# Expert weights loaded from the mixer's heads on, round 1's down weights ahead of the ranking, and the context's pieces some rounds later

## What is computed

```
for l in range(DEPTH):                        # first block, DEPTH = 2
    h = x * (1 + scale1) + shift1
    y = token_mixer(h, w_in[l], ..., w_out[l], cos, sin)
    x = layer_norm(ALPHA * x + gate1 * y, ln1_g[l], ln1_b[l])
    h = x * (1 + scale2) + shift2
    y = moe_ffn(h, router_w[l], router_bias[l], w_gate[l], w_up[l], w_down[l], ws_gate[l], ws_up[l], ws_down[l])
    x = layer_norm(ALPHA * x + gate2 * y, ln2_g[l], ln2_b[l])

def run_block(args):                          # in moe_ffn, for the tokens of one expert e
    e, toks, ws = args
    xb = x_pad[toks]
    hb = jax.nn.silu(xb @ w_gate[e]) * (xb @ w_up[e])
    return (hb @ w_down[e]) * ws[:, None]
```

## Time and profile before

| | |
|---|---|
| median of 3 runs | 2985.43 us (2981.14 to 2989.08) |
| the profiled execution | 2987.12 us, its span 2985.3 us |
| busy: PE, DVE, ACT, POOL | 2788.2, 1609.2, 766.0, 410.5 us |
| PE's chain of work that ended last | PE 75%, DVE 11%, DMA 9% of the span |
| moved by transfers | 717.28 MB, mean 240 GB/s |
| experts of layer 0 | about 281 to 794 us |
| experts of layer 1 | about 1044 to 1527 us |

### The profile page before, as it was taken

One profiled execution on the slowest core, in us unless ns is written; L12 is line 12 of the kernel. 1 busy time (PEld: TensorE's weight loads), 2 busy tenths in 40 slices (PEclk: granted clock), 3 DMA queues, 4 the chain that ended last, 5 costly groups with the idle time before them and its releaser, 6 DMA issues.

```text
span 2985.3 us, 65359 instructions
## 1 busy us (share of the span) xinstructions
PE 2788.2 (93%) x27428; PEld 2054.2 (69%) x27428; DVE 1609.2 (54%) x2814; ACT 766.0 (26%) x1408; POOL 410.5 (14%) x341
## 2 busy tenths in 40 slices
PE   7999999988989999998989899999998999899998
PEld 5768666655677856655567588844577888888973
DVE  3845333333463654444436478798757445555555
ACT  0122212121112133223213422200044424443210
POOL 1000000000000000000000036400023302444630
PEclk9999999999999999999999999999999999999999
DMA  9946999999984599999974035485430023001443
GB/s 392 374 184 239 407 395 410 391 421 420 408 336 143 221 391 418 414 407 420 420 283 155 1 129 172 168 314 191 141 120 4 4 91 135 4 18 32 156 168 113
DMA packets 102416, 717.28 MB, mean 240 GB/s; under 512 B 11648, under 2 KB 11936, under 8 KB 17888
## 3 DMA queue, kind: packets, MB, share of 16 engines
q1 hardware_dynamic: 98448, 700.03, 59.9%
q0 software_dynamic: 3664, 12.96, 1.3%
HBM read 710.06 MB, written 2.88 MB: 239 GB/s over the span
## 4 chain that ended last, share of the span: by engine, by line
PE 75%; DVE 11%; DMA 9%; ACT 3%; issue 2%; SPq 0%; POOL 0%; DVEq 0%; ACTq 0%; POOLq 0%
PE ps L229 16%; PE ps L1713 10%; PE ps L2267 9%; PE ps L2292 8%; DMA arena<-in_w_up 6%; DVE arena L162 5%; PE ps L3245 5%; PE ps L1742 5%; PE ps L2938 3%; PE ps L1810 2%; ACT arena L145 2%; PE ps L2660 1%; DMA arena<-in_w_in 1%; DVE arena L166 1%; DMA arena<-in_w_down 1%
## 5 line engine op out<-in xcount | busy, mean ns | idle before, releaser
L145 ACT ACTIVATE arena<-ps 128x512 f32<-128x512 f32 (+3 forms) x527 | 265.7, 504 | 1291.1 <-PE ps L229 276.6
L162 POOL TENSOR_TENSOR arena<-arena 128x512 f32<-128x512 f32 (+1 forms) x288 | 377.9, 1312 | 826.5 <-DVE arena L162 284.5
L229 PE MATMUL ps<-arena 128*128 128x256 f32 x2112 | 474.6, 385 | 16.0 <-DMA arena<-in_w_in 5.3
L229 PEld LDWEIGHTS ps<-arena 128*128 128x128 f32 x2112 | 402.5, 192 | 85.8 <-issue 11.2
L1713 PE MATMUL ps<-arena 128*32 128x256 f32 (+2 forms) x5120 | 395.2, 393 | 44.8 <-DMA arena<-in_w_up 33.8
L1713 PEld LDWEIGHTS ps<-arena 128*32 128x32 f32 (+2 forms) x5120 | 248.3, 121 | 194.5 <-issue 95.0
L162 DVE TENSOR_TENSOR arena<-ps,arena 128x256 f32<-128x256 f32 (+3 forms) x416 | 203.8, 490 | 236.9 <-PE ps L3245 88.4
L162 DVE TENSOR_TENSOR arena<-arena 128x512 f32<-128x512 f32 (+6 forms) x473 | 293.9, 621 | 61.0 <-PE ps L2292 36.0
L2267 PE MATMUL ps<-arena 128*128 128x256 f32 (+1 forms) x1792 | 298.5, 328 | 2.2 <-DVE arena L162 1.5
L2292 PE MATMUL ps<-arena 128*128 128x512 f32 x672 | 293.1, 593 | 2.5 <-DVE arena L162 2.5
L2267 PEld LDWEIGHTS ps<-arena 128*128 128x128 f32 x1792 | 270.0, 191 | 29.7 <-DVE arena L171 3.3
(11 more groups left out here) (292 smaller groups left out, 2908.4 us busy)
## 6 DMA issues: line engine op xcount, KB each, us to landing
arena<-in_w_gate SPq DMA_DIRECT2D x128, 1024.0 KB, 12.7
arena<-in_w_up SPq DMA_DIRECT2D x128, 1024.0 KB, 13.9
arena<-in_w_down SPq DMA_DIRECT2D x128, 1024.0 KB, 12.8
arena<-in_mlp SPq DMA_DIRECT2D x80, 1024.0 KB, 4.8
arena<-in_w_ada SPq DMA_DIRECT2D x48, 1024.0 KB, 13.1
arena<-in_ada SPq DMA_DIRECT2D x48, 1024.0 KB, 5.1
arena<-in_w_in SPq DMA_DIRECT2D x30, 1024.0 KB, 12.9
arena<-in_w_rkv SPq DMA_DIRECT2D x20, 1024.0 KB, 4.9
```

What stands on the lines that cost most here:

```text
L145: self.e.activation(out, in_, func, bias=bias, scale=scale, **more).then_inc(*self.done(key))
L162: self.e.tensor_tensor(out, a, b, op).then_inc(*self.done(key))
L229: ins = pe.matmul(out, a, b, start=start and i == 0, stop=stop and i == len(pairs) - 1)
```

## The change

- **Ahead of the end of the mixer.** The mixer's data is laid out anew, so that what lies in places 9 to 11 (`hT`, `PP`, `PT`, `qT`) is dead after the last pair of attention heads. After the first tile of `w_out`, `mixer_sp` now issues the shared gate and `FRONT`: both gates and both ups of round 0 and both gates of round 1, seven tiles, into places 5 to 11 (`load_apart` picks the place and leaves the ring's turn where it was). Places 9 to 11 wait for the heads' last values (`("mixer", l), "values", 3, 0`). The other three `w_out` tiles follow. Places 11 (both layers) and 10 (layer 0) are used for this alone and then go to the context.
- **Ahead of the ranking.** Then come the downs of round 0, the ups of round 1 and the downs of round 1; the last were issued in turn 1 before, behind the gates of round 2.
- **The context.** Its rows are loaded behind the gates of round 4 in layer 0 and not ahead of the ranking. In layer 1 the kept keys and values (0.5 and 0.25 MiB) follow the gates of round 2, and the kept queries (1 MiB) those of round 3. In layer 0 the squaring and scaling of the rows stand at the end of turn 3. `PIECE_ROUNDS` moves qkv 4 from turn 2 to 5, qkv 5 from 6 to 8, qkv 0 from 7 to 9, qkv 1 from 10 to 12, and the jobs between them alike; `HEAD_ROUNDS` starts in turn 3 instead of 1.

```diff
         def load(sp, key, used, src, parts=None, also=()):
...
-            if i >= NRING + NAPART and weights.fresh is not None:
-                ended(sp, weights.fresh, "pe", "act", "dve")
-                weights.fresh = None
...
+        def load_apart(sp, i, key, used, src):
+            turn, weights.turn, size, weights.size = weights.turn, i, weights.size, len(tiles)
+            load(sp, key, used, src)
+            weights.turn, weights.size = turn, size
...
+        FRONT = [(name, r, e) for name, r in (("w_gate", 0), ("w_up", 0), ("w_gate", 1)) for e in places_of(r)]
...
                 load(sp, ("w_bb", l, hf), ("y", l, hf * 4 + 3), D["w_bb"][l, hf])
-            for i in range(4):
+            load(sp, ("w_out", l, 0), ("mixed", l, 0, 1), D["w_out"][l, 0])
+            for i in range(NRING + NAPART, NRING + NEXTRA):
+                weights.used[i] = [(("mixer", l), "values", 3, 0)]
+            load_apart(sp, NRING, ("ws_gate", l), ("shared gate", l), D["ws_gate"][l])
+            for i, (name, r, e) in enumerate(FRONT):
+                load_apart(sp, NRING + 1 + i, (name, l, e), (name[2:], l, r), expert_rows(sp, name, l, e))
+            for i in range(1, 4):
                 load(sp, ("w_out", l, i), ("mixed", l, i, 1), D["w_out"][l, i])
...
-        PIECE_ROUNDS = {1: [("rows", 0), ("rows", 1), ("rows", 2)], 2: [("rows", 3), ("qkv", 4)], 3: [("keys", 0), ("keys", 1)],
-                        6: [("qkv", 5)], 7: [("qkv", 0)], 9: [("queries", 0)], 10: [("qkv", 1)], 12: [("queries", 1)], 15: [("qkv", 2)],
-                        16: [("queries", 2)], 17: [("qkv", 3)], 18: [("queries", 3)]}
+        PIECE_ROUNDS = {4: [("rows", 0), ("rows", 1), ("rows", 2)], 5: [("rows", 3), ("qkv", 4)], 6: [("keys", 0), ("keys", 1)],
+                        8: [("qkv", 5)], 9: [("qkv", 0)], 10: [("queries", 0)], 12: [("qkv", 1)], 13: [("queries", 1)],
+                        15: [("qkv", 2)], 16: [("queries", 2)], 17: [("qkv", 3)], 18: [("queries", 3)]}
...
-        for a, p in enumerate((1, 3, 7, 10, 14, 16, 18, 21)):
-            q = {3: 6, 7: 9, 10: 12}.get(p, p + 1)
+        for a, (p, q) in enumerate(((3, 4), (6, 7), (9, 10), (12, 14), (15, 16), (17, 18), (19, 20), (21, 22))):
...
         def moe_sp(sp, l):
-            weights.size, weights.turn, weights.fresh = NRING + EXTRA[l], NRING, ("mixer", l)
-            load(sp, ("ws_gate", l), ("shared gate", l), D["ws_gate"][l])
+            weights.size, weights.turn = NRING + EXTRA[l], 0
             for p, new, _, _ in rounds(l):
...
-                if new is not None:
+                if new is not None and new > 1:
                     for e in places_of(new):
                         load(sp, ("w_gate", l, e), ("gate", l, new), expert_rows(sp, "w_gate", l, e))
...
+                if new == 3 and l:
+                    sp.wait_ge(*at["gate", l, 1])
+                    sp.dma_start(CX.rows, kept[:, 0:2048]).then_inc(*tables["rows"]("c queries kept", 16))
+                if new == 4 and not l:
+                    sp.wait_ge(*at["gate", l, 1])
+                    sp.dma_start(CX.rv, D["ctx"].rearrange("(t p) n -> p t n", p=128)).then_inc(*tables["rows"]("rows", 16))
                 early_sp(sp, l, p, (0,))
-                if p >= 0:
+                if p >= 0 and p != 1:
                     for e in places_of(p):
                         load(sp, ("w_down", l, e), ("yd", l, p, 1), expert_rows(sp, "w_down", l, e))
...
+                if p == 0:
+                    for e in places_of(1):
+                        load(sp, ("w_down", l, e), ("yd", l, 1, 1), expert_rows(sp, "w_down", l, e))
```

More of the change, by code:

```diff
@@ L939, in __init__ @@
                 self.Zv = self.Z.rearrange("p (t n) -> p t n", t=2)
+                self.norms = arena[:, 6144:8192]
                 self.GSv = self.GS.rearrange("p (m t) -> p m t", m=16)
@@ L1116, in mixer_act @@
                 ended(act, ("moe", l - 1), "pe", "dve")
+                act.wait_ge(*at["c kept"])
             act.wait_ge(*mods(0, l, 0, 1))
@@ L1152, in mixer_dve @@
                 ended(dve, ("moe", l - 1), "pe", "act")
+                dve.wait_ge(*at["c kept"])
             else:
@@ L1566, in moe_sp @@
                     ended(sp, ("mixer", l), "pe", "act", "dve")
-                    if l:
-                        sp.wait_ge(*at["c kept"])
-                        sp.dma_start(gates[:, 0:1024], kept[:, 2048:3072]).then_inc(*tables["rows"](None, 16))
-                        sp.dma_start(CX.rows, kept[:, 0:2048]).then_inc(*tables["rows"]("c queries kept", 16))
-                    else:
-                        sp.dma_start(CX.rv, D["ctx"].rearrange("(t p) n -> p t n", p=128)).then_inc(*tables["rows"]("rows", 16))
@@ L1573, in moe_sp @@
                     sp.wait_ge(*at["ids", l])
-                    if l:
-                        sp.wait_ge(*at["scores", l])
-                        sp.dma_start(rw, kept[:, 3072:3584]).then_inc(*tables["rows"]("c values kept", 16))
-                if new is not None:
+                if new is not None and new > 1:
                     for e in places_of(new):
                         load(sp, ("w_gate", l, e), ("gate", l, new), expert_rows(sp, "w_gate", l, e))
+                if new == 2 and l:
+                    sp.wait_ge(*at["c kept"])
+                    sp.dma_start(gates[:, 0:1024], kept[:, 2048:3072]).then_inc(*tables["rows"](None, 16))
+                    sp.wait_ge(*at["scores", l])
+                    sp.dma_start(rw, kept[:, 3072:3584]).then_inc(*tables["rows"]("c values kept", 16))
@@ L1852, in moe_act @@
                 gather(0, k)
-            if not l:
-                context_rows_act(act, do)
             for p, new, Q, ks in rounds(l):
@@ L1883, in moe_act @@
                 early_act(act, do, l, p, 2)
+                if p == 3 and not l:
+                    act.wait_ge(*at["gate", l, 1])
+                    context_rows_act(act, do)
             ln_act(act, do, ("moe", l))
@@ L2055, in moe_dve @@
                     do.ts(CX.sk, CX.sk, -1.0, None, ALU.mult, None)
-                if p < 0 and not l:
+                if p == 3 and not l:
                     context_rows_dve(dve, do)
```

19 lines of the change are left out of this document (11 added, 8 removed).

## The result

The kernel after takes 3005.99 us (median of 5 runs, 2998.96 to 3007.45) beside 2985.05 us of before; the ratio is 1.0065 (95% interval 1.0049 to 1.0081). It is slower by about 20 us. The profiled execution takes 3005.99 us, span 3004.2.

A forecast was written before the change was run, and what follows sets the result against it. The prediction took transfers to bound the ends of both expert phases. Layer 0 at +4 us and layer 1 at -1 us took the profiled 2987.1 to 2990.1, a median of 2988 us; 8 in 10 for 2974 to 2998.

The forecast's parts named there:

- What bounds the kernel now: Both expert phases end by transfers, not PE, at some 410 to 420 GB/s; one tile costs 2.50 us.
- What the loads gain: Ahead of layer 0's ranking: one tile more than before, -2.5 us; the front loads themselves cost nothing.
- the rival: "The early loads pay": both layers' downs leave the saturated stretch, no hole opens, layer 0's middle gives 6 us; about 2974, 20%.
- What the ring takes back: Layer 0, round 3: its third gate waits for the place of round 1's first down, a hole of +5.1 us.
- The sum of +2.6 us at round 3: Layer 0 up to round 3: -2.5 us from the loads and +5.1 us from the ring's hole.
- The middle of layer 0: Moved pieces and rows' scaling (1.6 us in turn 4) leave +2 us at round 12's third up, bounds -6 and +5.
- "+2" behind the shared expert: Layer 0: qkv 1 holds its place until about 549 us; round 13's downs and the next up come 2 us later.
- Layer 1: -1: Half a tile of lead gives -1.3 us, round 3's third up lands within 0.3 us of before; -1 us in all.
- half pair of heads less: Layer 1: less head work ahead of the shared expert may return 1 us.
- The sum: Whole kernel: 2987.1 + 4 - 1 = 2990.1 profiled, a median of 2988 us, ratio 1.001.
- The downs' place in the ring costs twice: Layer 1 also opens the full 5.1 us and turn 5's qkv delays PE to the end; +12, 2997 us, 15%.
- its own sign: That slower rival decides if round 3's third gate issues later than about 5 us after the queue ran dry.

The follow-up runs named there:

- b_twice4: Before with the sixteen matmuls of qkv 4 run twice in turn 2 (7.2 us more for PE); 1.0046 of before.
- b_twice5: Before with the matmuls of qkv 5 run twice in turn 6 (7.2 us more for PE); 1.0053 of before.
- a_front: After with the seven front tiles issued behind the last w_out tile instead of the first, in both layers; 1.0054 of before.
- best0: After with context rows or kept queries loaded early, one round 1 tile in place 10, places freed in PE's order, heads and later pieces as before; 1.0024 of before.
- a_order: a_rows with the same number of tiles ahead of the ranking in other places, so places behind it come free in PE's order; 1.0023 of before.
- a_rows: After with the context's rows in layer 0 loaded behind round 3's gates and scaled at the end of turn 2, one turn earlier; 1.0041 of before.
- b_pieces: Before with only PIECE_ROUNDS of after, so the context's pieces in layer 0 run some turns later; 1.0022 of before.
- a_downs: After with round 1's downs back in turn 1, behind the gates of round 2, in both layers; 1.0040 of before.
- b_heads: Before with only HEAD_ROUNDS of after, so the context's heads in layer 1 start in turn 3 instead of 1; 1.0018 of before.
- b_ring3: Before with the second block's ring of three places started at place 0 instead of 1, as in after; 0.9985 of before.
- b_less4: Before with qkv 4's product in turn 2 cut to one of eight parts (6.3 us less for PE, wrong results); 1.0014 of before.
- b_less5: Before with qkv 5's product in turn 6 cut to one of eight parts (6.3 us less for PE, wrong results); 1.0007 of before.

## Why the prediction was wrong

It said 2988 us, with 2974 to 2998 for 8 in 10, and no change; 3006 lies outside. By its steps:

- **What bounds the kernel now.** That "both phases end by transfers, not by PE" holds at their ends, but I carried it through layer 0. (The slices I read as 410 to 420 GB/s are 391 to 421.) b_twice4 and b_twice5 show 7.2 us of PE's work costing 10.4 and 7.2 us by 758 us. Before is balanced between the two up to 550 us.
- **What the loads gain.** Costing the front loads at nothing fits a_front, within its 7 us. One tile of lead fits best0, early by 0.5 to 3 us. The -2.5 us did not live to the end of layer 0. The Trainium skill's rule that I gave the rival (DMA: Bandwidth & Descriptors, Rules for kernel authors) brought no time here: in best0 the loads are issued as early as memory allows and the time is no shorter.
- **What the ring takes back.** Right in mechanism, and right in place for one standstill of two. SP's third gate of round 3, last of this row, goes at 305.55 + 11.97 = 317.5 us, with the transfers at rest from 314.7:

```profile
305.55 11.97 SPq L320 DMA_DIRECT2D arena<-in_w_gate  x3
```

  The forecast was 315, and the ranking is 2.1 us late. But my own walk has a gap before this one: four tiles behind the ranking land by 297.1 us, and the next is issued at 300.0 and lands at 304.8. I didn't charge it. After rests there too, 3.5 us at 299.5, so 6.8 us in the two; in 286 to 315 us it moves 87 GB/s less than before, 2.5 MB, which are 6.0 us at 420 GB/s. The sum of +2.6 us at round 3 came out as 6.5 by the count of tiles, of which 2.1 are the late ranking. For a_order against a_rows, in layer 0 alone, the profiles have 7.4 to 8.0 us where +5.1 was said.
- **The middle of layer 0** is the step that failed first and most. I said +2 us at round 12's third up, near 512 us, within -6 and +5; it lands 10.8 us late, and PE runs it at 520.85. The hole near 414 us came, 2.9 us long for the 4 I said. At that same tile b_pieces is 0.2 us early, a_order 1.8 early, a_rows 5.7 late, a_downs 7.3 and after 10.8, one profile each. So up to here the pieces' new places cost little (some 2.3 us, if the tile of qkv 1, which is still to come, is counted). The downs' place costs 7.5 us (a_rows less a_order) where 5.1 was said, and the late rows 5.1 us (after less a_rows) where 1.6 was said. Three things behind these sizes were wrong. PE's wait for the scaling was 2.97 us, not 1.6. PE waited 17.0 us for weights before 550 us, before 5.6 (of which 3.3 at round 12) and 4.1 mostly for a gather; I had priced such waits at nothing, because transfers end the phase. But b_twice4 and b_twice5 show that a delay of PE in these turns delays the places by its full length. The third is the clock: PE's busy time includes half-speed matmuls behind new waits. "+2" behind the shared expert came out as 5.7, and here the pieces do cost: b_pieces goes from 0.2 us early to 6.2 late between 510 and 566 us, 2.5 of it the tile of qkv 1.
- **Layer 1: -1.** Wrong sign. The wait for round 3's third up shows the hole that the kept data did not fill:

```profile
1108.06 3.64 PE L1761 MATMUL ps<-arena 128*32 128x512 f32 x32 [1.11 <-DMA arena<-in_w_down]
1115.27 3.20 PE L1732 MATMUL ps<-arena 128*32 128x256 f32 x32 [3.57 <-DMA arena<-in_w_up]
```

  It lands 19.1 us late, the ranking 16.9. Two us are the hole, not 0.3. (The lead takes 1.4 tiles for the 1.5 MiB of kept data; 1.5 gives the same half tile.) The "half pair of heads less" that was to return 1 us is part of the move that b_heads shows costing 5.4. Between the last tiles of the two layers after loses 8 to 9 us in all, and what these two don't cover stays open.
- **The sum** left out a term: where the ring stands after the experts, -4.5 us (b_ring3).
- **The rivals.** "The downs' place in the ring costs twice" had the right side, but by its own sign it should not have decided: the third gate went 2 to 3 us after the transfers came to rest, not more than 5. That turn 5's qkv makes PE late to the end is not shown (b_pieces has it there and is not late at round 12). Its 12 us were still 8 short.

The measured parts, b_pieces 6.6, b_heads 5.4, downs 7.5 (after less a_downs), late rows 7.2 (after less a_rows), ring position -4.5, sum to 22 us against 20. They were not measured independently, and each is known to 4 to 7 us only, so this agreement may be luck.

## What to carry to other kernels

Taking work out of a stretch in which another limit stands close behind gained almost nothing here, and adding work where the engine sets the pace cost its length, so price both ends of a move: add the work once more at each, and leave it out at each. Then look through the whole profile for waits that the edit itself made elsewhere, since each of the four kernels with a product repeated or shortened had one of 4.5 to 4.9 us here. A ring that frees in order wants its tiles in the order of use; a prefetch that is used later than its neighbour holds back all behind it. Loads into an idle stretch gained nothing where the bound behind them was how many tiles fit.

## What the hardware showed that I had not expected

- **A wait can cost more than its length.** The granted clock was at 1.2 GHz (0.50) behind the wait of 5.75 us and at 2.4 GHz (1.00) again at 363.4: down products of 3.64 us took 5.07, 5.34 and 6.36 us behind waits of 2.65, 2.97 and 5.75 us, and 3.64 with the wait filled. The Trainium skill (TensorE: Matmul & The Clock Gate, Part 1) has the clock halved by idleness and released by activity, and varying from run to run; this case's traces agree.
- **The same program's stalls cost differently in each execution.** In the unchanged layer 0 of before and b_ring3 round 4's gate took 5.35 and 6.11 us behind the same wait, where others of its form take 3.66 (first before's row, then b_ring3's):

```profile
353.40 5.35 PE L1713 MATMUL ps<-arena 128*32 128x256 f32 x64 [3.87 <-issue]
```

```profile
353.55 6.11 PE L1713 MATMUL ps<-arena 128*32 128x256 f32 x64 [3.88 <-issue]
```

  A slow product near 512 us was there in b_ring3 alone. Layer 0 ended 3.3 us apart in the two with no change in its program; that the clock is all of this is not shown.
- **A wait for nothing that the profile shows.** b_twice4, b_twice5, b_less4 and b_less5 each had one more of them than all other kernels, 4.5 to 4.9 us long and hundreds of us behind the edit.
